# Every large SBUF buffer of a two-block transformer kernel placed at a multiple of 2048 bytes

## The chip, the cores and the metric

The kernel runs on one core of a Trainium2 chip. The metric is the device time of one launch in microseconds, median of the runs shown.

## The reference, cut to what matters

Two transformer blocks work on x of 512 rows by 1024 features in float32. The first has two layers: a norm, a projection, a gated spatial unit beside causal differential attention, an output projection, then a feed-forward part with a three-tap convolution. The second has one layer: a modulated norm, a projection, a linear recurrence beside sparse attention, an output projection, then a feed-forward part with a squared relu.

```python
for l in range(DEPTH):                                   # first block, DEPTH = 2
    proj = rmsnorm(h, attn_norm[l]) @ w_in[l]            # 1024 -> 2560
    mixed = concat([sgu_mixer(u, v_sgu, ...), diff_attention(q, k, v_att, ...)])
    h = h + mixed @ w_out[l]                             # 1024 -> 1024
    h = h + conv_ffn(rmsnorm(h, ffn_norm[l]), w_up[l], conv_w[l], conv_b[l], w_down[l])   # 1024 -> 2*2816, 2816 -> 1024
h = rmsnorm(h, final_norm)
y = hybrid_mixer(modulate(rms_norm(h, g), sh1, sc1), w_in_2, ..., w_out_2)                # second block
h = h + (1 + g1) * rms_norm(y, post_norm_mix_2)
y = square(relu(modulate(rms_norm(h, g), sh2, sc2) @ w_ff1_2)) @ w_ff2_2                  # 1024 -> 4096 -> 1024
return h + (1 + g2) * rms_norm(y, post_norm_mlp_2)
```

## The kernel before, in words

**Tiling.** Features lie on the 128 partitions, the 512 rows of x along a partition. So an activation tile is 128 x 512 float32, 2048 bytes of a partition. h holds the eight tiles of the residual stream.

**The product.** Every large matrix product is made of three matmuls in the reduced float32 format (`product`, L2024 to L2028): each operand is split into a high part and a low remainder, and high x high, high x low and low x high are summed in PSUM. Mostly the weight is the stationary operand (128 x 128) and the activation is streamed (512 columns).

```python
pe.matmul(out, l_hi, r_hi, start=start, stop=False)          # L2026
pe.matmul(out, l_hi, r_lo, start=False, stop=False)          # L2027
return pe.matmul(out, l_lo, r_hi, start=False, stop=stop)    # L2028
```

The profile names both inputs of a matmul in the order of the alphabet: `ps<-n_lo,w_hi` streams n_lo over the stationary w_hi. In some projections (forms `ps<-w_hi,n_hi`) the activation is stationary and the weight is streamed.

**The split operands.** n_hi and n_lo (8 tiles each) hold the normed activation that enters a projection or the upper half of a feed-forward part. x_hi and x_lo (4 tiles each) hold the gated result of the spatial unit, which enters the first half of the out-projection (`outs`; its second half `outa` reads n_hi and n_lo), and the hidden activation that enters the lower half of a feed-forward part.

**Weights.** SyncE loads a stripe of weights (1 MB or 512 KB) into raw0 or raw1, asked for when the stripe before it in that buffer has been split. A stripe has four quarters. ScalarE copies a quarter to w_hi (`hi`, L885), then POOL makes w_lo = raw - w_hi (`lo`, L848), into one of four slots. ScalarE runs three quarters ahead of PE (LOOK = 3), and a slot comes free when PE has done the quarter four before.

**The loops.** The feed-forward parts are hardware loops: 11 groups in each layer of the first block, 8 in the second. A turn does `up` for one group (four PSUM banks, 24 matmuls on n_hi and n_lo into each) and `down` for the group before (eight output tiles into four banks, 6 matmuls on x_hi and x_lo into each, 12 in the second block). VectorE and ScalarE turn the upper results into the hidden activation in zc (rb), ScalarE splits it to x_hi (L933), VectorE to x_lo (L1389), and VectorE adds the lower results to h (L1736) or y, which lies in zy (L1976).

**The layout.** `sb(name, shape)` takes SBUF from a stack: a buffer starts where the one before it ended, rounded up to 32 bytes, and a buffer opened in a `with ExitStack() as part` gives its place back, so that the next one lies over it. 1152 bytes of a partition are taken before the first buffer. Worked out from the shapes, a buffer's start counted past the last multiple of 2048, and past the last multiple of 64:

| buffers | before | of 64 | after | of 64 |
|---|---|---|---|---|
| raw0, raw1, w_hi, w_lo, h, n_hi, n_lo, zb, zc | 1152 | 0 | 0 | 0 |
| zd | 1152 | 0 | 0 | 0 |
| x_hi, x_lo, za, zy | 1696 | 32 | 0 | 0 |
| tb, cb_hi, sq | 128 | 0 | 0 | 0 |
| ss | 320 | 0 | 0 | 0 |
| blkw, rotF, cb_lo | 1632 | 32 | 0 | 0 |
| const | 320 | 0 | 448 | 0 |
| ones | 1920 | 0 | 1024 | 0 |

The buffers named are in `build` (L451 to L498 before the change). Tiles within the large buffers step by 2048 bytes, weight tiles within a slot by 512.

Of the kernel before, what the change touches and what calls it, by code (L numbers as in the profile page):

```python
# [19 lines left out]
F32 = mybir.dt.float32  # L20
F32R = mybir.dt.float32r
# [5 lines left out]
P = 128  # L27
S = 512
NT = S // P
D = 1024  # L30
DT = D // P
DEPTH = 2
HALF = D // 2
HT = HALF // P
HEADS = 4
FF = 2816
FG = FF // 256
# [70 lines left out]
NCONST = C_QSCALE + HEADS2 // 2  # L108
# [336 lines left out]
def build(nc, a):  # L445
# [7 lines left out]
    with ExitStack() as ctx:  # L453
        def sb(name, shape, dt=F32, where=ctx):
            return where.enter_context(nc.sbuf_tensor(name, shape, dt))
# [2 lines left out]
            return ctx.enter_context(nc.semaphore(name))  # L458


        raw = [sb(f"raw{i}", [P, 4096]) for i in range(2)]
        w_hi = sb("w_hi", [P, 4, 1024], F32R)
        w_lo = sb("w_lo", [P, 4, 1024], F32R)
# [4 lines left out]
        n_lo = sb("n_lo", [P, DT, S], F32R)  # L468
        zb = sb("zb", [P, 4096])
        zc = sb("zc", [P, 2048])  # L470
        zd = sb("zd", [P, 3328])
        with ExitStack() as part:
            tb = sb("tb", [P, 3, S], F32, part)
        cb_hi = sb("cb_hi", [P, 16, 64], F32R)
        sb("rest_of_tb", [P, S])
        sq = sb("sq", [P, 2, S])
        rt = sb("rt", [P, HEADS * NT])
        rstd = sb("rstd", [P, HEADS * NT + 1])
        ms = sb("ms", [P, 2 * NT])
        ss = sb("ss", [P, 2, S])  # L480
        const = sb("const", [P, NCONST])
        ones = sb("ones", [P, P])
        cols = sb("cols", [P, 6, P])
        par = sb("par", [P, DEPTH, FG * 16])
        cpar = sb("cpar", [P, 17])
        small = sb("small", [P, 48])
        more = sb("more", [P, 144])
        blkw = sb("blkw", [P, 2, HT, P])
        with ExitStack() as part:
            rotF = sb("rotF", [P, 2, S], F32, part)  # L490
        cb_lo = sb("cb_lo", [P, 16, 64], F32R)
        fgw = sb("fgw", [P, DT, 2])
        cw2 = [sb(f"cw2_{i}", [P, 2, P]) for i in range(2)]
        with ExitStack() as part:
            za = sb("za", [P, 4096], F32, part)
        x_hi = sb("x_hi", [P, 4, S], F32R)
        x_lo = sb("x_lo", [P, 4, S], F32R)
        zy = sb("zy", [P, 4096])  # L498
        banks = ctx.enter_context(nc.psum_tensor("ps", [P, 8 * S], F32))
        ps = [banks[:, i * S:(i + 1) * S] for i in range(8)]  # L500

# [2129 lines left out]
```

## Time and profile before

| what | value |
|---|---|
| median of 3 runs | 1925.64 us (1924.38 to 1927.17) |
| profiled execution, span from its first to its last instruction | 1919.2 us |
| what lies around that span, against the median | 6.4 us |
| TensorE busy | 1834.7 us, 96% of the span |
| VectorE, ScalarE, POOL busy | 54%, 41%, 46% |
| mean granted TensorE clock | 0.975 |
| HBM read | 180.42 MB, 95 GB/s over the span |

The profiled execution's time on the runs' clock is not listed apart; the median stands for it, and the span is what rows of the trace add up to. PE is TensorE's matmuls and PEld its weight loads, which overlap. Matmuls overlap one another as well: the start of the next, not the end, tells what one costs. A busy PE is not PE at its peak.

### The profile page before, as it was taken

How to read it: one execution, taken by the hardware profiler on the slowest of the kernel's cores; microseconds unless marked ns; L12 is line 12 of the kernel's file. 1: busy time of each engine (PE TensorE's matmuls, PEld its weight loads, DVE VectorE, ACT ScalarE, POOL GpSimd, SP SyncE). 2: the span in 40 equal slices, each digit the busy share in tenths (PEclk: the TensorE clock that was granted, in tenths of full speed). 3: DMA queues.
4: the chain of work that ended last, by engine and by line, in shares of the span. 5: the costliest groups of instructions: out<-in, count | busy, mean ns of one | idle time of the engine just before them, and what ended most of it. 6: DMA issues, size and time to landing. Idle time of an engine off the chain costs nothing.

```text
span 1919.2 us, 25690 instructions
## 1 busy us (share of the span) xinstructions
PE 1834.7 (96%) x8675; PEld 1466.2 (76%) x8675; DVE 1027.1 (54%) x1800; ACT 779.3 (41%) x1244; POOL 891.9 (46%) x1158
## 2 busy tenths in 40 slices
PE   7999999999999999999999999999988899999996
PEld 5767788888887877778888888867556778888885
DVE  4687556566656347576656654554675542222223
ACT  4434433333335334353333333485665342222223
POOL 5443345565555543255656554357112335555541
PEclk9999999999999999999999999899999789999998
DMA  7221224443322222124444323133001212223211
GB/s 240 89 88 44 77 67 153 142 153 127 135 88 88 90 87 74 36 78 142 153 142 153 135 95 110 51 105 126 8 1 45 88 44 88 87 92 120 94 44 44
DMA packets 102018, 183.43 MB, mean 96 GB/s; under 512 B 6794, under 2 KB 66748, under 8 KB 99900
## 3 DMA queue, kind: packets, MB, share of 16 engines
q1 hardware_dynamic: 101772, 181.80, 27.1%
q8 instruction: 40, 0.66, 0.1%
q10 hardware_dynamic: 176, 0.73, 0.1%
q14 instruction: 30, 0.25, 0.0%
HBM read 180.42 MB, written 2.10 MB: 95 GB/s over the span
## 4 chain that ended last, share of the span: by engine, by line
PE 87%; DVE 6%; ACT 3%; issue 3%; POOL 1%; DMA 0%; DVEq 0%; SPq 0%; ACTq 0%; POOLq 0%
PE ps L2026 26%; PE ps L2028 25%; PE ps L2027 25%; PE ps L2283 1%; DVE ss L1374 1%; PE ps L2052 1%; PE ps L2564 1%; PE ps L2220 1%; DVE n_lo L1393 1%; PE ps L2274 1%; DVE zy L1898 1%; PE ps L2537 1%; POOL w_lo L848 1%; PE ps L2513 1%; PE ps L2061 1%
## 5 line engine op out<-in xcount | busy, mean ns | idle before, releaser
L848 POOL TENSOR_TENSOR w_lo<-raw,w_hi 128x256 fp32r<-128x256 f32 (+1 forms) x1148 | 889.0, 807 | 989.1 <-ACT w_hi L885 988.9
L2026 PE MATMUL ps<-n_hi,w_hi 128*128 128x512 f32 x1432 | 573.6, 401 | 7.7 <-DVE n_lo L1411 3.2
L2028 PE MATMUL ps<-n_hi,w_lo 128*128 128x512 f32 x1432 | 561.3, 392 | 0.0
L2027 PE MATMUL ps<-n_lo,w_hi 128*128 128x512 f32 x1432 | 560.8, 392 | 0.0
L885 ACT ACTIVATE w_hi<-raw 128x1024 fp32r<-128x1024 f32 (+2 forms) x331 | 310.0, 944 | 302.5 <-PE ps L2028 183.8
L2026 PEld LDWEIGHTS ps<-n_hi,w_hi 128*128 128x128 f32 x1432 | 270.1, 189 | 69.2 <-issue 10.5
L2027 PEld LDWEIGHTS ps<-n_lo,w_hi 128*128 128x128 f32 x1432 | 270.2, 189 | 58.5 <-issue 4.3
L2028 PEld LDWEIGHTS ps<-n_hi,w_lo 128*128 128x128 f32 x1432 | 269.8, 188 | 59.0 <-issue 0.7
L2026 PE MATMUL ps<-x_hi,w_hi 128*128 128x512 f32 x672 | 272.5, 406 | 4.7 <-DVE x_lo L1389 4.7
L2027 PE MATMUL ps<-x_lo,w_hi 128*128 128x512 f32 x672 | 268.3, 399 | 0.0
L2028 PE MATMUL ps<-x_hi,w_lo 128*128 128x512 f32 x672 | 267.9, 399 | 0.0
L1718 DVE TENSOR_TENSOR ps<-ps,sq 128x512 f32<-128x512 f32 x88 | 61.4, 700 | 192.1 <-PE ps L2028 189.7
L2026 PEld LDWEIGHTS ps<-x_hi,w_hi 128*128 128x128 f32 x672 | 127.9, 190 | 39.1 <-DVE x_lo L1389 5.3
L1088 ACT ACTIVATE zc<-ps,cpar 128x512 f32<-128x512 f32 x88 | 68.2, 775 | 210.9 <-DVE ps L1718 210.9
L2028 PEld LDWEIGHTS ps<-x_hi,w_lo 128*128 128x128 f32 x672 | 127.9, 190 | 31.6
L1736 DVE TENSOR_TENSOR h<-h,ps 128x512 f32<-128x512 f32 x176 | 111.3, 679 | 75.3 <-PE ps L2028 75.3
L2027 PEld LDWEIGHTS ps<-x_lo,w_hi 128*128 128x128 f32 x672 | 128.2, 191 | 29.6 <-issue 0.5
L1976 DVE TENSOR_TENSOR zy<-zy,ps 128x512 f32<-128x512 f32 x64 | 41.4, 683 | 140.3 <-PE ps L2028 140.3
L1971 DVE TENSOR_TENSOR zc<-zc 128x512 f32<-128x512 f32 x32 | 23.8, 745 | 123.7 <-ACT zc L1322 123.7
L933 ACT ACTIVATE x_hi<-zc 128x512 fp32r<-128x512 f32 x76 | 43.2, 624 | 70.6 <-PE ps L2028 68.6
L1725 DVE SCALAR_TENSOR_TENSOR zc<-ps,cpar,zc 128x510 f32<-128x510 f32 x88 | 65.9, 749 | 3.1
L1389 DVE TENSOR_TENSOR x_lo<-zc,x_hi 128x512 fp32r<-128x512 f32 x76 | 65.6, 910 | 0.2
(285 smaller groups left out, 1886.5 us busy)
## 6 DMA issues: line engine op xcount, KB each, us to landing
raw<-in_w_up SPq DMA_DIRECT2D x44, 1024.0 KB, 6.8
raw<-in_w_ff SPq DMA_DIRECT2D x32, 1024.0 KB, 6.3
raw<-in_w_in SPq DMA_DIRECT2D x26, 1024.0 KB, 7.1
zb<-in_ada_w SPq DMA_DIRECT2D x16, 1536.0 KB, 7.9
raw<-in_w_down SPq DMA_DIRECT2D x44, 512.0 KB, 4.0
raw<-in_w_out SPq DMA_DIRECT2D x12, 1024.0 KB, 6.0
raw<-in_w_in SPq DMA_DIRECT2D x4, 512.0 KB, 10.1
za<-in_x SPq DMA_DIRECT2D x4, 512.0 KB, 7.9
```

The source lines that it names most:

```text
L848: last = pool.tensor_tensor(parts[0][:, c], parts[1][:, c], parts[2][:, c], ALU.subtract)
L885: act.activation(split_quarter(st.kind, w_hi, g % 4, q), raw_quarter(st.kind, raw[st.index % 2], q), ACT.Copy).then_inc(whi_ready, 1)
L933: act.activation(dst, src, ACT.Copy).then_inc(hi_ready, 1)
L1088: act.activation(rb[t], ps[t][:, :], ACT.Identity, bias=cpar[:, 4 * t + 3:4 * t + 4], scale=cpar[:, 4 * t + 2:4 * t + 3]).then_inc(conv_be ...
L1389: dve.tensor_tensor(lo_, src, hi_, ALU.subtract).then_inc(lo_ready, 1)
L1718: dve.tensor_tensor(ps[t][:, :], ps[t][:, :], factor, ALU.mult).then_inc(up_scaled, 1)
L1725: dve.scalar_tensor_tensor(rb[t][:, 2:S], ps[t][:, 0:S - 2], cpar[:, 4 * t:4 * t + 1], rb[t][:, 2:S], ALU.mult, ALU.add).then_inc(free[t], 1)
L1736: dve.tensor_tensor(h[:, m, :], h[:, m, :], ps[4 + m % 4][:, :], ALU.add)\
L1976: dve.tensor_tensor(y[:, m, :], y[:, m, :], ps[4 + m % 4][:, :], ALU.add)\
L2026: pe.matmul(out, l_hi, r_hi, start=start, stop=False)
L2027: pe.matmul(out, l_hi, r_lo, start=False, stop=False)
L2028: return pe.matmul(out, l_lo, r_hi, start=False, stop=stop)
```

## The change

The seven small buffers of parameters and of norm results are opened first, with a filler of 88 floats that nothing uses: 64 + 96 + 32 + 96 + 192 + 64 + 352 = 896 bytes after the 1152, so raw0 starts at 2048. After them come the buffers whose sizes are multiples of 2048 bytes, then zd and the remaining parameters. za with x_hi and x_lo, and zy, move ahead of tb. Sizes, pairs that share a place, and all instructions stay.

```diff
@@ -458,6 +458,13 @@
             return ctx.enter_context(nc.semaphore(name))
 
 
+        rt = sb("rt", [P, HEADS * NT])
+        rstd = sb("rstd", [P, HEADS * NT + 1])
+        ms = sb("ms", [P, 2 * NT])
+        cpar = sb("cpar", [P, 17])
+        small = sb("small", [P, 48])
+        fgw = sb("fgw", [P, DT, 2])
+        sb("to_tiles", [P, 88])
         raw = [sb(f"raw{i}", [P, 4096]) for i in range(2)]
         w_hi = sb("w_hi", [P, 4, 1024], F32R)
         w_lo = sb("w_lo", [P, 4, 1024], F32R)
@@ -468,34 +475,28 @@
         n_lo = sb("n_lo", [P, DT, S], F32R)
         zb = sb("zb", [P, 4096])
         zc = sb("zc", [P, 2048])
-        zd = sb("zd", [P, 3328])
+        with ExitStack() as part:
+            za = sb("za", [P, 4096], F32, part)
+        x_hi = sb("x_hi", [P, 4, S], F32R)
+        x_lo = sb("x_lo", [P, 4, S], F32R)
+        zy = sb("zy", [P, 4096])
         with ExitStack() as part:
             tb = sb("tb", [P, 3, S], F32, part)
         cb_hi = sb("cb_hi", [P, 16, 64], F32R)
         sb("rest_of_tb", [P, S])
         sq = sb("sq", [P, 2, S])
-        rt = sb("rt", [P, HEADS * NT])
-        rstd = sb("rstd", [P, HEADS * NT + 1])
-        ms = sb("ms", [P, 2 * NT])
         ss = sb("ss", [P, 2, S])
-        const = sb("const", [P, NCONST])
-        ones = sb("ones", [P, P])
-        cols = sb("cols", [P, 6, P])
-        par = sb("par", [P, DEPTH, FG * 16])
-        cpar = sb("cpar", [P, 17])
-        small = sb("small", [P, 48])
-        more = sb("more", [P, 144])
         blkw = sb("blkw", [P, 2, HT, P])
         with ExitStack() as part:
             rotF = sb("rotF", [P, 2, S], F32, part)
         cb_lo = sb("cb_lo", [P, 16, 64], F32R)
-        fgw = sb("fgw", [P, DT, 2])
+        zd = sb("zd", [P, 3328])
         cw2 = [sb(f"cw2_{i}", [P, 2, P]) for i in range(2)]
-        with ExitStack() as part:
-            za = sb("za", [P, 4096], F32, part)
-        x_hi = sb("x_hi", [P, 4, S], F32R)
-        x_lo = sb("x_lo", [P, 4, S], F32R)
-        zy = sb("zy", [P, 4096])
+        ones = sb("ones", [P, P])
+        cols = sb("cols", [P, 6, P])
+        par = sb("par", [P, DEPTH, FG * 16])
+        more = sb("more", [P, 144])
+        const = sb("const", [P, NCONST])
         banks = ctx.enter_context(nc.psum_tensor("ps", [P, 8 * S], F32))
         ps = [banks[:, i * S:(i + 1) * S] for i in range(8)]
```

## Rows read from the trace of the kernel before

**Rows 1.** The page: busy time by engine (share, instructions), and the chain that ended last.

```profile
PE 1834.7 (96%) x8675; PEld 1466.2 (76%) x8675; DVE 1027.1 (54%) x1800; ACT 779.3 (41%) x1244; POOL 891.9 (46%) x1158
...
PE 87%; DVE 6%; ACT 3%; issue 3%; POOL 1%; DMA 0%; DVEq 0%; SPq 0%; ACTq 0%; POOLq 0%
PE ps L2026 26%; PE ps L2028 25%; PE ps L2027 25%; PE ps L2283 1%; DVE ss L1374 1%; PE ps L2052 1%; PE ps L2564 1%; PE ps L2220 1%; DVE n_lo L1393 1%; PE ps L2274 1%; DVE zy L1898 1%; PE ps L2537 1%; POOL w_lo L848 1%; PE ps L2513 1%; PE ps L2061 1%
```

**Rows 2.** Table of stretches, the three feed-forward loops: us, busy (instructions), clock, DMA.

```profile
core 0: us, PE busy (x) PEld busy (x) DVE busy (x) ACT busy (x) POOL busy (x), PEclk, DMA share, GB/s
255.00:590.00 335.00, 335.00 (x1463) 273.42 (x1462) 206.94 (x272) 122.07 (x167) 182.90 (x243) 1.00 0.35 121
845.00:1190.00 345.00, 344.54 (x1508) 281.47 (x1507) 210.91 (x279) 125.07 (x172) 188.27 (x248) 1.00 0.36 124
1550.00:1875.00 325.00, 325.00 (x1415) 265.00 (x1413) 80.17 (x118) 93.99 (x120) 170.44 (x236) 1.00 0.23 84
sum 1005.00, PE 1004.54 PEld 819.89 DVE 498.03 ACT 341.13 POOL 541.62; mean PE 334.85 PEld 273.30 DVE 166.01 ACT 113.71 POOL 180.54
```

**Rows 3.** Groups of PE's instructions: line, form xcount | busy us, mean ns | idle before.

```profile
L2026 PE MATMUL ps<-n_hi,w_hi 128*128 128x512 f32 x1432 | 573.6, 401 | 7.7 <-DVE n_lo L1411 3.2 <-DVE n_lo L1389 2.2 <-issue 1.4
L2028 PE MATMUL ps<-n_hi,w_lo 128*128 128x512 f32 x1432 | 561.3, 392 | 0.0
L2027 PE MATMUL ps<-n_lo,w_hi 128*128 128x512 f32 x1432 | 560.8, 392 | 0.0
L2026 PE MATMUL ps<-x_hi,w_hi 128*128 128x512 f32 x672 | 272.5, 406 | 4.7 <-DVE x_lo L1389 4.7
L2027 PE MATMUL ps<-x_lo,w_hi 128*128 128x512 f32 x672 | 268.3, 399 | 0.0
L2028 PE MATMUL ps<-x_hi,w_lo 128*128 128x512 f32 x672 | 267.9, 399 | 0.0
L2026 PE MATMUL ps<-w_hi,n_hi 128*128 128x512 f32 x128 | 52.2, 408 | 5.5 <-issue 3.7 <-DVE zd L1470 1.8
L2027 PE MATMUL ps<-w_lo,n_hi 128*128 128x512 f32 x128 | 51.4, 402 | 0.0
L2028 PE MATMUL ps<-w_hi,n_lo 128*128 128x512 f32 x128 | 51.4, 402 | 0.0
```

**Rows 4.** Timeline of PE, second block's loop: start us, duration us, engine, line, operation.

```profile
1698.35 0.40 PE L2026 MATMUL ps<-n_hi,w_hi 128*128 128x512 f32 x1
...
1719.92 0.39 PE L2028 MATMUL ps<-n_hi,w_lo 128*128 128x512 f32 x1
1720.15 0.40 PE L2026 MATMUL ps<-x_hi,w_hi 128*128 128x512 f32 x1
...
1742.32 0.40 PE L2028 MATMUL ps<-x_hi,w_lo 128*128 128x512 f32 x1
```

**Rows 5.** Timeline of PE, out-projection of layer 0: on x, then on n.

```profile
204.89 0.39 PE L2027 MATMUL ps<-x_lo,w_hi 128*128 128x512 f32 x1
...
207.22 0.39 PE L2028 MATMUL ps<-x_hi,w_lo 128*128 128x512 f32 x1
...
221.07 0.39 PE L2026 MATMUL ps<-n_hi,w_hi 128*128 128x512 f32 x1
...
231.72 0.39 PE L2028 MATMUL ps<-n_hi,w_lo 128*128 128x512 f32 x1
```

**Rows 6.** Two stretches at the halved clock: table of stretches, then PE's timeline.

```profile
211.00:214.00 3.00, 3.00 (x8) 2.42 (x9) 0.00 (x0) 0.26 (x1) 0.00 (x0) 0.50 0.00 0
1488.00:1490.00 2.00, 2.00 (x6) 1.52 (x6) 1.97 (x4) 1.58 (x2) 1.58 (x2) 0.50 0.00 0
...
212.03 0.63 PE L2028 MATMUL ps<-x_hi,w_lo 128*128 128x512 f32 x1
...
213.31 0.63 PE L2028 MATMUL ps<-x_hi,w_lo 128*128 128x512 f32 x1
...
1488.11 0.63 PE L2028 MATMUL ps<-n_hi,w_lo 128*128 128x512 f32 x1
...
1489.82 0.63 PE L2026 MATMUL ps<-n_hi,w_hi 128*128 128x512 f32 x1
```

**Rows 7.** Groups of VectorE and ScalarE whose operands lie at different places.

```profile
L1736 DVE TENSOR_TENSOR h<-h,ps 128x512 f32<-128x512 f32 x176 | 111.3, 679 | 75.3 <-PE ps L2028 75.3
L1976 DVE TENSOR_TENSOR zy<-zy,ps 128x512 f32<-128x512 f32 x64 | 41.4, 683 | 140.3 <-PE ps L2028 140.3
...
L908 ACT ACTIVATE sq<-h 128x512 f32<-128x512 f32 x28 | 17.3, 621 | 7.9 <-DVE h L1602 4.7 <-DVE ss L1374 3.1
L908 ACT ACTIVATE sq<-zy 128x512 f32<-128x512 f32 x14 | 8.7, 626 | 15.8 <-DVE zy L1976 9.9 <-DVE zy L1942 5.8
...
L933 ACT ACTIVATE x_hi<-tb 128x512 fp32r<-128x512 f32 x8 | 5.1, 634 | 21.6 <-DVE tb L1593 21.6
L933 ACT ACTIVATE n_hi<-tb 128x512 fp32r<-128x512 f32 x16 | 10.1, 631 | 25.4 <-DVE tb L1608 21.0 <-DVE tb L1874 2.8 <-DVE tb L1419 1.4
...
L1389 DVE TENSOR_TENSOR x_lo<-tb,x_hi 128x512 fp32r<-128x512 f32 x8 | 5.5, 684 | 0.0
L1389 DVE TENSOR_TENSOR n_lo<-tb,n_hi 128x512 fp32r<-128x512 f32 x16 | 11.9, 743 | 1.4 <-ACT n_hi L933 1.3
```

**Rows 8.** POOL: its group on the page, its wait (us, times, longest), its timeline.

```profile
L848 POOL TENSOR_TENSOR w_lo<-raw,w_hi 128x256 fp32r<-128x256 f32 (+1 forms) x1148 | 889.0, 807 | 989.1 <-ACT w_hi L885 988.9
...
POOL w_lo L848 <- ACT w_hi L885: 988.9, 215, 37.9
...
1711.09 2.83 POOL L848 TENSOR_TENSOR w_lo<-raw,w_hi 128x256 fp32r<-128x256 f32 x4 [1.52 <-ACT w_hi L885]
1716.53 2.83 POOL L848 TENSOR_TENSOR w_lo<-raw,w_hi 128x256 fp32r<-128x256 f32 x4 [2.62 <-ACT w_hi L885]
```

**Rows 9.** The chain in order of time, its first transfer; PE's wait for it.

```profile
1.32 6.68 DMA za<-in_x
...
PE ps L2158 <- DMA za<-in_x: 8.1, 1, 8.1
```

## The prediction, made before the result was known

> **What bounds the kernel now.** Four views, in this order. The page's busy shares and chain [rows 1]: TensorE (PE) is busy 1834.7 of the span's 1919.2 us and makes 87% of the chain that ended last; three source lines alone, the three matmuls of one compensated float32 product (L2026 to L2028), make 76% of it. The table of stretches [rows 2]: in the two feed-forward loops of the first block and in the one of the second, 1005 us together, PE is busy for 1004.5 us at a granted clock of 1.00, while POOL, the next busiest, has 541.6 us. So in those stretches the time is the number of matmuls times the distance from one start to the next, and no wait stands in it. The groups of product matmuls [rows 3] split this work by what they stream: 4680 stream n_hi, n_lo or, with n as the stationary side, w_hi and w_lo (3 x 1432 + 3 x 128); 2016 stream x_hi or x_lo (3 x 672). Of the three costliest forms the first kind shows 401, 392 and 392 ns for one, the second 406, 399 and 399. These durations overlap, so they are only a hint. The timeline gives the real price [rows 4]: in one turn of the second block's loop 96 matmuls on n start from 1698.35 to 1719.92 us, 21.57 us over 95 steps, 227.1 ns each; the next 96, on x, start from 1720.15 to 1742.32 us, 22.17 us over 95 steps, 233.4 ns each. Both have 512 columns and a 128x128 stationary tile, with nothing idle between.
>
> What differs is where the streamed operand lies. By the layout, n_hi, n_lo, w_hi and w_lo begin 1152 bytes past a multiple of 2048, which is a multiple of 64 (and 128); x_hi and x_lo begin at 1696, which is 32 past a multiple of 64. Two other differences could stand behind the 6.3 ns: the upper loop half sums 24 matmuls into a PSUM bank, the lower half 6 or 12. Here the trace has a control [rows 5]: the two halves of the out-projection use the same weight layout and 12 matmuls per bank, one on x, one on n. On x, 10 steps take 2.33 us (233 ns); on n, 47 steps take 10.65 us (226.6 ns). So the price goes with the operand, not with the grouping.
>
> **The change, part by part.** (1) The streamed x_hi and x_lo move from 32 past a multiple of 64 to a multiple of 2048. Their distance in phase to w_hi and w_lo becomes zero, just as n_hi's is now, so the nearest row for them is n's 227.1 ns. Gain: 233.4 - 227.1 = 6.3 ns, times 2016 = 12.7 us. The page's means give a second road: 5 + 7 + 7 = 19 ns for each triple, times 672 = 12.8 us. Subtractions: at the halved clock (0.50 in these windows) x steps by 1.28 us in 3 (427 ns) and n by 1.71 in 4 (427 ns) [rows 6], so the few dozen x matmuls that run there gain nothing, some 0.2 us; and the 192 x matmuls of the two attention stages stand in short runs between softmax steps, where VectorE and ScalarE set part of the pace, so I take off half of their 1.2 us. Left: 12.7 - 0.2 - 0.6 = 11.9 us.
>
> (2) Everything else that is large moves from 1152 to 0 past a multiple of 2048. No row has n at another phase. Bounds: nothing lower than the halved clock's 427 ns divided by two, 213.5 ns, is thinkable for 512 columns, which would be 13.6 ns less on each of 4680; upward, n could cost what x costs now, 6.3 ns more. I take 0, because 1152 and 0 are both multiples of 64 and 128, and n keeps its phase to the weights.
>
> (3) The engines beside PE. VectorE's sum with a PSUM operand takes 679 ns on h and 683 on zy, which lies at 1696 like x; ScalarE's square 621 from h, 626 from zy; its copy 634 into x_hi and 631 into n_hi; VectorE's difference 684 for x_lo, 743 for n_lo [rows 7]. So these engines see no price in the place beyond 5 ns, and the parameters, read a few columns at a time, are taken at 0. POOL's part takes 2.83 us per quarter of weights, while PE spends 24 x 227 ns = 5.4 us on one, and it waits for ScalarE before nearly each [rows 8]; even 1 us more per quarter stays hidden there. If that cover were gone, a w_lo late by 0.1 us in each of 287 quarters (1148 instructions, four to one) would cost 29 us, but after this change a lower-half quarter of 12 x 227 ns = 2.7 us is only 0.08 us shorter than now, with three quarters of run-ahead kept. Late next, if anything, is w_lo in that half: the change takes 48 x 6.3 = 0.3 us from a turn, which is no wait.
>
> (4) The transfers. All but the first are asked for stripes ahead. At the start PE waits 8.1 us for x in za, of which 6.68 us is the transfer [rows 9]. za moves from 160 past a multiple of 256 to a multiple of it. No row has another phase; bounds by the rows are a tenth of 6.68 us each way, and I take 0.
>
> Sum: -11.9 us. Against the profiled execution's own span that is 1919.2 - 11.9 = 1907.3 us. The median of the runs, 1925.64, lies 6.4 us above the span, and that part (launch and end) is untouched: 1913.7 us. A measurement of this kernel can tell about 0.2%, 3.9 us, from no change.
>
> **The rivals.** *No effect of address.* The 6.3 ns would come from the work, say the PSUM banks' order or VectorE beside the lower half. Against it stands the control [rows 5]; for it, that the x runs there are short. Time: 1925.6 us. The Trainium skill (SBUF — State Buffer, the note on cachelines) speaks for this rival: a consecutive read pays only for each new line of 16 bytes, and 1696 and 1152 are both multiples of 16; by that rule nothing changes. The trace's 233.4 beside 227.1 ns do not agree with it.
>
> *More than x.* The 13.6 ns between 227.1 and 213.5 would also be an address price, which the full 2048 removes from all 6696: 4680 x 13.6 = 64 us and 2016 x 19.9 = 40 us, so 1822 us. For it: at the halved clock no such surcharge shows. Against: n's streams and w's, a run of 512 and one of 128 columns at different offsets, all sit at 227 already. The Trainium skill (TensorE: Matmul & The Clock Gate, Back-to-back issue gap) gives N/2.4 + 2.5 ns for isolated matmuls, 216 ns here; by that the sum would be an estimated 1925.6 - 87 = 1838 us. The trace shows 227.1 with a weight load before each matmul.
>
> *Slower: a common phase.* Now x stands apart from the weights and the other buffers; afterwards PE's stream, its weight load and the other engines' operands all begin at one phase, where they may collide. Place: the product matmuls; price: n's 4680 at x's 6.3 ns more, 29.5 us, with x kept at 233.4: 1955 us. It decides from 11.9 / 4680 = 2.5 ns per n matmul. Against it: n_hi, raw, h and w_hi share one phase already, and they are the fast ones.
>
> **How the numbers follow.** Forecast 0.82 (two roads to its term and a control); no effect 0.08; more 0.05; slower 0.05. Forecast's own spread: 6.3 ns may be 5 (some of the x steps follow a stall) or 7.1, plus 0.7 us of the transfer and 1.5 us of scatter: 1909 to 1918. Stretched to take in half-effects, 1907 to 1920. Faster by over 0.2%: 0.82 and 0.05, less a little for a half-effect, 0.86; within: 0.09; slower: 0.05.
>
> **What would show it.** In the profile of the changed kernel the x block of a turn should step by 227 ns as the n block does, L2027 and L2028 on x should have n's mean of about 392 ns, and a turn of the second block's loop, 44.2 us from one n block's start to the next's (192 steps), should take 43.6. n's step and the means of POOL, VectorE and ScalarE should stay within 1%. The prediction is wrong if x keeps 233 ns, if n's step moves by more than 1 ns, or if a wait for w_lo or x_lo appears inside the loops.

## The result, and the profile of the changed kernel

The changed kernel took 1909.86 us in the median (4 runs, 1907.88 to 1910.30), the kernel before 1926.41 us beside it (4 runs, 1924.38 to 1928.69): a ratio of 0.9913, 95% interval [0.9896, 0.9930], or 16.5 us less. The forecast was 1913.7 us in 1907 to 1920. A second comparison, with nine runs of the changed kernel and fourteen of the one before, gave a little less: 1914.68 against 1927.0 us, 0.9938 [0.9917, 0.9959], 12.3 us. Both hold; why they differ, and how much of either is the layout's, comes with the experiments.

The page of the changed kernel, same parts as [rows 1], and its groups of product matmuls beside [rows 3]. All source lines are one further down, so L2026 to L2028 are now L2027 to L2029; the chain's first three entries are still these.

```profile
span 1908.2 us, 25690 instructions
PE 1823.5 (96%) x8675; PEld 1465.1 (77%) x8675; DVE 1031.8 (54%) x1800; ACT 779.6 (41%) x1244; POOL 884.4 (46%) x1158
...
PE 87%; DVE 6%; ACT 3%; issue 3%; POOL 1%; DMA 0%; DVEq 0%; SPq 0%; ACTq 0%; POOLq 0%
...
L849 POOL TENSOR_TENSOR w_lo<-raw,w_hi 128x256 fp32r<-128x256 f32 (+1 forms) x1148 | 881.5, 803 | 985.4 <-ACT w_hi L886 983.7
L2027 PE MATMUL ps<-n_hi,w_hi 128*128 128x512 f32 x1432 | 572.9, 400 | 7.7 <-DVE n_lo L1412 3.2
L2029 PE MATMUL ps<-n_hi,w_lo 128*128 128x512 f32 x1432 | 561.2, 392 | 0.0
L2028 PE MATMUL ps<-n_lo,w_hi 128*128 128x512 f32 x1432 | 560.7, 392 | 0.0
...
L2027 PE MATMUL ps<-x_hi,w_hi 128*128 128x512 f32 x672 | 269.0, 400 | 4.7 <-DVE x_lo L1390 4.7
L2028 PE MATMUL ps<-x_lo,w_hi 128*128 128x512 f32 x672 | 264.2, 393 | 0.0
L2029 PE MATMUL ps<-x_hi,w_lo 128*128 128x512 f32 x672 | 264.0, 393 | 0.0
```

The same instructions, 11.0 us less span (1919.2 to 1908.2), and PE's busy time is 11.2 us less. The x groups went from 406, 399 and 399 ns to 400, 393 and 393; the n groups stayed where they were. POOL did not slow down (807 to 803 ns). Since a matmul's duration overlaps the next one's, the price is read from the distance between starts, in the timeline of PE in the second block's loop, as in [rows 4]: 96 starts on x, then 96 on n, then the next block on x and the next on n.

```profile
1711.53 0.39 PE L2027 MATMUL ps<-x_hi,w_hi 128*128 128x512 f32 x1
...
1733.06 0.39 PE L2029 MATMUL ps<-x_hi,w_lo 128*128 128x512 f32 x1
1733.29 0.39 PE L2027 MATMUL ps<-n_hi,w_hi 128*128 128x512 f32 x1
...
1754.82 0.39 PE L2029 MATMUL ps<-n_hi,w_lo 128*128 128x512 f32 x1
...
1776.81 0.39 PE L2027 MATMUL ps<-n_hi,w_hi 128*128 128x512 f32 x1
```

Each block takes 21.53 us over 95 steps, 226.7 ns, on x as on n. Before, it was 233.4 on x and 227.1 on n. A turn, from one n block's start to the next's, takes 43.52 us (1733.29 to 1776.81) where it took 44.20.

The table of stretches answers to [rows 2]; the stretch of the second block is set a little earlier, since the program has reached it earlier.

```profile
core 0: us, PE busy (x) PEld busy (x) DVE busy (x) ACT busy (x) POOL busy (x), PEclk, DMA share, GB/s
255.00:590.00 335.00, 335.00 (x1469) 274.71 (x1468) 208.80 (x273) 122.28 (x168) 181.20 (x244) 1.00 0.35 122
840.00:1180.00 340.00, 340.00 (x1495) 278.93 (x1493) 212.43 (x278) 125.44 (x171) 182.71 (x246) 1.00 0.35 124
1540.00:1860.00 320.00, 320.00 (x1414) 264.96 (x1413) 83.66 (x123) 95.59 (x122) 167.74 (x233) 1.00 0.24 85
sum 995.00, PE 995.00 PEld 818.60 DVE 504.89 ACT 343.32 POOL 531.65; mean PE 331.67 PEld 272.87 DVE 168.30 ACT 114.44 POOL 177.22
```

PE is busy in every microsecond of it. That hides something: 1463 instructions in 335 us became only 1469, 0.4% more. With the x third of them 2.9% quicker one would look for about 1%. The timeline shows what is in the way. PE with its weight loads, and VectorE, in a turn of the first block's loop, at the 25th matmul on x (column in brackets: idle before it and what ended that).

```profile
290.15 1.87 DVE L1737 TENSOR_TENSOR h<-h,ps 128x512 f32<-128x512 f32 x3
...
290.56 0.39 PE L2029 MATMUL ps<-x_hi,w_lo 128*128 128x512 f32 x1
290.88 0.19 PEld L2027 LDWEIGHTS ps<-x_hi,w_hi 128*128 128x128 f32 x1 [0.35 <-DVE h L1737]
290.88 0.50 PE L2027 MATMUL ps<-x_hi,w_hi 128*128 128x512 f32 x1
...
291.22 0.39 PE L2028 MATMUL ps<-x_lo,w_hi 128*128 128x512 f32 x1
```

The same place in the kernel before:

```profile
290.21 1.87 DVE L1736 TENSOR_TENSOR h<-h,ps 128x512 f32<-128x512 f32 x3
...
290.77 0.40 PE L2028 MATMUL ps<-x_hi,w_lo 128*128 128x512 f32 x1
...
290.94 0.19 PEld L2026 LDWEIGHTS ps<-x_hi,w_hi 128*128 128x128 f32 x1 [0.21 <-DVE h L1736]
291.01 0.44 PE L2026 MATMUL ps<-x_hi,w_hi 128*128 128x512 f32 x1
...
291.29 0.39 PE L2027 MATMUL ps<-x_lo,w_hi 128*128 128x512 f32 x1
```

Here the fifth output tile starts in the PSUM bank of the first, and VectorE must first have added that bank to h. VectorE's chain did not get quicker, PE did: the two steps around this matmul are 0.32 and 0.34 us after the change, 0.24 and 0.28 before, instead of 0.227 each. PE still counts as busy, because the last matmul's modelled end covers the gap. Summed over the 20 turns of both loops the excess of these two steps over 227 ns is 4.08 us, against 0.94 before: 3.1 us of the gain were given back in a wait that the prediction said would not come. The steps right behind it are longer too (236, 231, 233 and 231 ns as medians of the turns, then 227 again), which brings the loss near 4 us.

The account by stage, from the starts of the same instructions in both traces: the two loops of the first block, each with the last group of `down` behind it, 3.3 us less each, the second block 4.4, the attention stages and the start 0 within 0.2 us. From the steps: 1922 x matmuls at full clock by 6.0 ns (233.4 to 227.35, short stalls included) are 11.6 us; n's 4477 by 0.2 ns are 0.9; less 3.1 that is 9.4 us.

The rest of the 11.0 us is the clock. Of the first block's 3.3 us the ten turns of a loop give only 1.5 to 1.6; the last group behind them gives 1.7, of which its own shorter steps are at most 0.3. There, behind some 3 us of small matmuls of a norm, PE ran on at the halved clock in the profiled execution of the kernel before (the third number from the right is the granted clock):

```profile
597.00:599.00 2.00, 2.00 (x6) 1.52 (x6) 0.00 (x0) 0.00 (x0) 0.88 (x2) 0.50 0.00 0
1187.00:1189.00 2.00, 2.00 (x5) 1.63 (x6) 0.00 (x0) 0.00 (x0) 1.18 (x2) 0.50 0.00 0
```

and at the full clock in that of the changed kernel:

```profile
595.50:597.50 2.00, 2.00 (x10) 1.63 (x9) 0.00 (x0) 0.00 (x0) 0.84 (x2) 1.00 0.08 5
1182.50:1184.50 2.00, 2.00 (x10) 1.67 (x9) 0.00 (x0) 0.00 (x0) 0.87 (x2) 1.00 0.07 6
```

These two places are worth 2.9 us; behind the second block's loop the halved stretch is longer in the changed kernel, which costs it 1.0. With the 9.4 that makes 11.3, beside the 11.0 measured. In its second profile the changed kernel is at the halved clock behind the second loop as well (0.50 from 1190.50 to 1192.50 us), so this part differs between executions of one kernel and is not shown to come from the layout. About 9 of the 11.0 us are the layout's.

### The profile page after: what moved, and what is told of

The parts are those of the page before. It is cut to its first block, busy times and chain, and to the rows that moved or that the text cites. A ratio compares the mean times of both kernels' runs of the same rounds, so it can differ in the third digit from the quotient of the medians.

```text
span 1908.2 us, 25690 instructions
## 1 busy us (share of the span) xinstructions
PE 1823.5 (96%) x8675; PEld 1465.1 (77%) x8675; DVE 1031.8 (54%) x1800; ACT 779.6 (41%) x1244; POOL 884.4 (46%) x1158
## 4 chain that ended last, share of the span: by engine, by line
PE 87%; DVE 6%; ACT 3%; issue 3%; POOL 1%; DMA 0%; DVEq 0%; SPq 0%; ACTq 0%; POOLq 0%
PE ps L2027 26%; PE ps L2028 25%; PE ps L2029 25%; PE ps L2284 1%; DVE ss L1375 1%; PE ps L2053 1%; PE ps L2565 1%; DVE n_lo L1394 1%; PE ps L2221 1%; PE ps L2275 1%; DVE zy L1899 1%; PE ps L2538 1%; POOL w_lo L849 1%; PE ps L2514 1%; PE ps L2062 1%
## 5 line engine op out<-in xcount | busy, mean ns | idle before, releaser
L2027 PE MATMUL ps<-n_hi,w_hi 128*128 128x512 f32 x1432 | 572.9, 400 | 7.7 <-DVE n_lo L1412 3.2
L2029 PE MATMUL ps<-n_hi,w_lo 128*128 128x512 f32 x1432 | 561.2, 392 | 0.0
L2028 PE MATMUL ps<-n_lo,w_hi 128*128 128x512 f32 x1432 | 560.7, 392 | 0.0
L2027 PEld LDWEIGHTS ps<-n_hi,w_hi 128*128 128x128 f32 x1432 | 270.2, 189 | 69.0 <-issue 10.5
L2028 PEld LDWEIGHTS ps<-n_lo,w_hi 128*128 128x128 f32 x1432 | 270.1, 189 | 58.1 <-issue 4.3
L2029 PEld LDWEIGHTS ps<-n_hi,w_lo 128*128 128x128 f32 x1432 | 269.7, 188 | 58.3 <-issue 0.8
L2027 PE MATMUL ps<-x_hi,w_hi 128*128 128x512 f32 x672 | 269.0, 400 | 4.7 <-DVE x_lo L1390 4.7
L2028 PE MATMUL ps<-x_lo,w_hi 128*128 128x512 f32 x672 | 264.2, 393 | 0.0
L2029 PE MATMUL ps<-x_hi,w_lo 128*128 128x512 f32 x672 | 264.0, 393 | 0.0
L2027 PEld LDWEIGHTS ps<-x_hi,w_hi 128*128 128x128 f32 x672 | 127.7, 190 | 38.4 <-DVE h L1737 7.1
L2029 PEld LDWEIGHTS ps<-x_hi,w_lo 128*128 128x128 f32 x672 | 127.6, 190 | 27.4
L2028 PEld LDWEIGHTS ps<-x_lo,w_hi 128*128 128x128 f32 x672 | 127.6, 190 | 25.8 <-issue 0.5
L1390 DVE TENSOR_TENSOR x_lo<-zc,x_hi 128x512 fp32r<-128x512 f32 x76 | 69.8, 964 | 0.2
```

Source lines behind the costliest of these rows:

```text
L1390: dve.tensor_tensor(lo_, src, hi_, ALU.subtract).then_inc(lo_ready, 1)
```

## The experiments

In these experiments fillers in the layout change, or the place of one addition in VectorE's order, or both; each kernel does the whole computation. "Distance" is the start of the streamed operand in a partition minus the start of the weights, modulo 256 bytes. Before, it was 0 for n and 32 for x (1696 - 1152 = 544 = 2 x 256 + 32).

**How firm is the 16.5 us.** The changed kernel again, in nine runs.

> The changed kernel itself once more, to measure the size. If the gain is only the shorter step of x (some 2000 matmuls by 6 ns, less a wait), it is 11 to 12 us, ratio 0.994. If the first comparison's 16.5 us are real, a second cause exists beside the step of x and this comparison gives 15 to 18 us again, ratio 0.991 to 0.992.

It gave 1914.68 us (1906.94 to 1921.25, 9 runs) against 1927.0 (1921.52 to 1931.73, 14 runs), ratio 0.9938 [0.9917, 0.9959]. The runs scatter by more than they did in the first comparison, and they do so with the granted clock: the 9 runs go from 1906.94 us at a mean clock of 0.981 to 1921.25 at 0.971. Over the 67 runs of this study that list a clock and have a fellow run, each kernel about its own mean, one thousandth of mean clock goes with 1.4 us (scatter left about that line: 1.4 us). Set to a clock of 0.975 by this slope, an estimate, the kernel before takes 1922.8 +- 0.3 us and the changed one 1914.4 +- 0.5 here, 1912.2 +- 0.7 in the first comparison. At equal clock, then, the layout is worth 8 to 11 us, about the 9.4 of the account; the rest is that the changed kernel happened to run, or was made to run, at a clock of 0.974 to 0.977 in the mean, the other at 0.971 to 0.973. Which of the two is left open; the slowest layouts below ran at 0.975 to 0.977, so the clock does not simply follow x's step.

**Is it the place or the distance.** Three layouts. In the first, the kernel before with eight words in front of x, x lies at 1728, a multiple of 64, and everything else stays:

```diff
         cw2 = [sb(f"cw2_{i}", [P, 2, P]) for i in range(2)]
+        sb("pad", [P, 8])
         with ExitStack() as part:
```

> The kernel before with 32 bytes of filler ahead of za: x_hi, x_lo, za and zy start at 1728 past a multiple of 2048 (a multiple of 64, not of 128), all else stays at 1152. Theory A (x's start past a multiple of 64 is the whole cause): x steps by 227 ns and the time is that of the changed kernel within 0.1%. Theory B (the full 2048, or 128, is needed): x keeps 233 ns and the time that of the kernel before. Theory C (more than x): x steps by 227 ns and the time lies between the two, some 5 us above the changed kernel.

In the second, the changed kernel with every large buffer at 32 past a multiple of 2048, distances 0:

```diff
-        sb("to_tiles", [P, 88])
+        sb("to_tiles", [P, 96])
```

> The changed kernel with every large buffer 32 bytes further, so that weights, n and x share one phase, 32 past a multiple of 64. If the place itself counts, n and x both step by 233 ns: 6696 matmuls by 6.3 ns, 40 us slower than the changed kernel. If only the distance in phase between the streamed and the stationary operand counts, both step by 227 ns and nothing changes.

In the third, the changed kernel with the weights alone moved by 32 bytes; x, n and all else stay on multiples of 2048:

```diff
+        sb("pad0", [P, 8])
         w_hi = sb("w_hi", [P, 4, 1024], F32R)
         w_lo = sb("w_lo", [P, 4, 1024], F32R)
+        sb("pad1", [P, 8])
```

> The changed kernel with 32 bytes of filler ahead of w_hi and 32 behind w_lo: the weights start 32 past a multiple of 64, n, x and all else at a multiple of 64. If the distance between the streamed and the stationary operand counts, every product that streams n or x is 32 off: 6312 matmuls by 6.5 ns, about 40 us slower than the changed kernel, steps of 233 ns on n and on x. If only the streamed operand's own place counts (against the run with all buffers at 32), steps stay at 227 ns.

Measured: 1916.25 us (6 runs), 0.9944 [0.9926, 0.9962] for the first; 1913.09 (4 runs), 0.9924 [0.9899, 0.9948] for the second; 1949.1 (2 runs), 1.0114 [1.0076, 1.0151] for the third. The timelines of PE say what happened to the step. x at a multiple of 64 with the weights at 1152:

```profile
1714.66 0.40 PE L2027 MATMUL ps<-x_hi,w_hi 128*128 128x512 f32 x1
...
1736.42 0.39 PE L2029 MATMUL ps<-x_hi,w_lo 128*128 128x512 f32 x1
```

Everything at 32:

```profile
1714.69 0.39 PE L2027 MATMUL ps<-x_hi,w_hi 128*128 128x512 f32 x1
...
1736.23 0.39 PE L2029 MATMUL ps<-x_hi,w_lo 128*128 128x512 f32 x1
```

The weights alone at 32, first the block on x, then the one on n:

```profile
1698.19 0.40 PE L2029 MATMUL ps<-x_hi,w_hi 128*128 128x512 f32 x1
...
1720.35 0.39 PE L2031 MATMUL ps<-x_hi,w_lo 128*128 128x512 f32 x1
1720.59 0.40 PE L2029 MATMUL ps<-n_hi,w_hi 128*128 128x512 f32 x1
...
1742.75 0.40 PE L2031 MATMUL ps<-n_hi,w_lo 128*128 128x512 f32 x1
```

Over 95 steps these are 21.76 us (229.1 ns), 21.54 us (226.7), and 22.16 us on both x and n (233.3). The second says that the place of an operand does not count: x at 32 past a multiple of 64 is as quick as anywhere. The third says that the distance does: x and n, both on multiples of 2048, became slow because the weights moved, and the kernel is 22 us slower than the one before with an alignment that looks nearly perfect. The first says that 64 is not the unit: a multiple of 64 still pays 2.4 ns.

**What the unit is.** Six more layouts. x was put 16 bytes, 128 bytes and 256 bytes further in the changed kernel (a filler of 32 or 64 words in front of za; the 16 bytes by a slice of a larger buffer); in two kernels, which also have the earlier addition of the experiment after this one, n was moved as well; and last the kernel before got a filler of 224 bytes, to bring x to 768 bytes past the weights' phase:

```diff
         cw2 = [sb(f"cw2_{i}", [P, 2, P]) for i in range(2)]
+        sb("pad", [P, 56])
         with ExitStack() as part:
```

> The changed kernel with za, x_hi and x_lo 16 bytes further (zy and what follows 64 further). The rule of 16-byte lines gives 227 ns a step for x. Lines of 64 bytes, or any dependence on the distance to the weights, give 230 to 236 ns.

> The changed kernel with 128 bytes of filler ahead of za: x is a multiple of 128 away from the weights' phase, but not of 256. The distance of 64 gave 229 ns. If the period is 128, x steps by 227 ns here; if it is longer (256, 512), by 228 to 231 ns; a step below 226.7 ns would be a better place than the common phase.

> As the run with 128 bytes, with 256: 227 ns if the period is 256 or less, above 228 if it is longer.

> On top of the run that adds first: n_hi and n_lo 192 bytes past the weights' phase, x_hi and x_lo 224. Distances so far: 0 and 256 gave steps of 226.7 ns, 16 gave 231.6, 32 gave 233.4, 64 gave 229.1, 128 gave 233.2, and weights 32 ahead of the streamed operand (a distance of 224) 233.3. If the distance within 256 bytes decides, x steps by 233 ns here. For n at 192: by symmetry with 64, 229 ns; a step near 213 ns would be a better place than the common phase.

> As before with n at 96 and x at 160. By symmetry the two give about the same step, between 229 and 234 ns. A step below 226.7 would overturn that the common phase is best.

> The kernel before with 224 bytes of filler ahead of za and nothing else: x_hi and x_lo start at 1920 past a multiple of 2048, a distance of 768 = 3 x 256 from the weights' phase, while everything else stays at 1152. If the distance within 256 bytes is the whole cause, x steps by 226.7 ns, the wait at the fifth output tile is 4 us in all, and the time is that of the changed kernel within the scatter (12 us under the kernel before at equal clock it would be 8 to 11). If the round places themselves give something, the changed kernel stays some us faster.

Times, in that order: 1922.71, 1923.93, 1907.98, 1947.81 and 1950.66 us (one run each) and 1916.51 us (5 runs) against 1926.32, 0.9946 [0.9932, 0.9960]. Blocks on x in the timeline of PE at 16, 128 and 256 bytes, each from its own kernel. At 16, where x is a slice of the buffer x_all:

```profile
1722.55 0.39 PE L2028 MATMUL ps<-x_all,w_hi 128*128 128x512 f32 x1
...
1744.55 0.40 PE L2030 MATMUL ps<-x_all,w_lo 128*128 128x512 f32 x1
```

At 128:

```profile
1723.16 0.40 PE L2028 MATMUL ps<-x_hi,w_hi 128*128 128x512 f32 x1
...
1745.33 0.39 PE L2030 MATMUL ps<-x_hi,w_lo 128*128 128x512 f32 x1
```

At 256:

```profile
1709.19 0.39 PE L2028 MATMUL ps<-x_hi,w_hi 128*128 128x512 f32 x1
...
1730.72 0.39 PE L2030 MATMUL ps<-x_hi,w_lo 128*128 128x512 f32 x1
```

22.00, 22.17 and 21.53 us: 231.6, 233.4 and 226.6 ns. All layouts together, x's or n's mean step in the second block's loop:

| distance, bytes mod 256 | step, ns | kernels |
|---|---|---|
| 0 (0, 256 and 768) | 226.7 | changed, all at 32, x at 256, filler of 224 |
| 16 | 231.6 | x at 16 |
| 32 | 233.4 | before |
| 64 | 229.1 | x at 64 |
| 96 | 233.3 | n at 96 |
| 128 | 233.3 | x at 128 |
| 160 | 234.2 | x at 160 |
| 192 | 233.3 | n at 192 |
| 224 | 233.3 | x at 224; weights at 32 |

So the step is at its lowest where stream and weights begin at the same place modulo 256 bytes; 16 bytes away it costs 4.9 ns more, and most other distances cost the 6.6 ns that the kernel before paid. One value between is quicker than its neighbours, 64, with 229.1. And since the filler of 224 bytes does to x's step all that the change does, 226.7 ns, nothing of the change's other moves was needed for it.

The forms that stream the weights over a stationary n (`ps<-w_hi,n_hi`) check the table, since there the distance has the opposite sign. With n at 96 it is 160, and their full-speed steps take 233.7 to 234.3 ns in every stretch, as x's at 160. With n at 192 it is 64, and two of the three long stretches take 228.9 ns, as x's at 64, but the third, from 673.0 to 695.2 us, 233.3. So the 160 repeats, and 64 is not always the quicker value. What in the chip makes this distance count is not shown by any of these runs, and distances that are no multiple of 16 were not tried.

**The wait for the bank.** If the new wait is VectorE's first add coming late, it must vanish when that add stands earlier in VectorE's order. In the changed kernel it stood behind the last product of the convolution, which itself waits for ScalarE; now it stands ahead of that product:

```diff
-                def conv_steps(j):
+                def conv_steps(j, between=None):
...
+                        if i == 1 and between is not None:
+                            between()
                         dve.wait_ge(free[2 * i + 1], n0[2 * i + 1] + j + 1)
...
-                        conv_steps(j)
-                        down_steps(gq + 4 + 8 * (j - 1))
+                        conv_steps(j, lambda: down_steps(gq + 4 + 8 * (j - 1), None, range(1)))
+                        down_steps(gq + 4 + 8 * (j - 1), None, range(1, DT))
```

> The changed kernel, with VectorE's first addition of the lower half's result (the one that frees the bank of the fifth output tile) moved ahead of its last product of the convolution part, in the two loops of the first block. If the wait of PE at the fifth output tile, about 0.2 us in each of 20 turns, is for VectorE's first addition, it goes and the time falls by 3 to 4 us. If it is for something else (weights), it stays and nothing changes or the later x_hi costs something.

> The changed kernel with the first addition moved ahead, once more: 4 us under the changed kernel at equal granted clock, ratio to the kernel before 0.990 to 0.993, and about 4 us under the run with 224 bytes of filler of the same call.

The two comparisons gave 1912.38 us (6 runs), 0.9910 [0.9889, 0.9932], and 1911.51 us (5 runs) against 1926.32, 0.9930 [0.9916, 0.9943]. The timeline of the second, at the same place of the turn:

```profile
288.71 0.68 DVE L1738 TENSOR_TENSOR h<-h,ps 128x512 f32<-128x512 f32 x1
289.31 0.68 DVE L1732 TENSOR_TENSOR zc<-zc 128x512 f32<-128x512 f32 x1
289.91 2.04 DVE L1738 TENSOR_TENSOR h<-h,ps 128x512 f32<-128x512 f32 x3
...
290.23 0.39 PE L2030 MATMUL ps<-x_hi,w_lo 128*128 128x512 f32 x1
...
290.46 0.39 PE L2028 MATMUL ps<-x_hi,w_hi 128*128 128x512 f32 x1
...
290.69 0.39 PE L2029 MATMUL ps<-x_lo,w_hi 128*128 128x512 f32 x1
```

The first add, now ahead of the convolution's product (zc<-zc), begins 1.75 us before the 25th matmul (290.46), where in the changed kernel it began 0.73 before it (290.15 and 290.88), and PE steps by 0.23 us. From one such matmul to that of the next turn it is 33.03 us in the kernel before, 32.87 in the changed one and 32.64 here, as means over the turns of both loops (the first: 291.01 to 324.03, 290.88 to 323.76, 290.46 to 323.10): of the 0.39 us that a turn of the first block can gain, the changed kernel got 0.16, and the wait with the longer steps behind it costs it 0.23, 4.7 us in 20 turns. The excess of the two steps alone over the 20 turns is 0.0 us in both profiles with the earlier addition, against 4.08 in the changed kernel, 4.06 in its second profile and 4.11 with the 224-byte filler. Against the kernels with the wait on the same chips the medians fell by 2.3 us (1914.68 to 1912.38) and by 5.0 (1916.51 to 1911.51); the intervals of the ratios still overlap, so the times alone do not settle it. At a clock of 0.975 it is 4.2 us (1914.4 to 1910.2) and 5.5 (1915.0 to 1909.5), which agrees with the 4.7 us of the turns within the error of about 0.8. The mechanism is shown by the timelines. This is the quickest version: at equal clock 12.6 to 13.3 us below the kernel before.

## Why the prediction was right, and where its steps were not

**(1) x's step: size and sign right, the cause misnamed.** Forecast 6.3 ns on each of 2016; measured 6.7 in the second block's loop and 6.0 over all full-speed steps, 11.6 us. The control of [rows 5] was good: operand, not grouping. But the prediction explained the 6.3 ns by x beginning 32 past a multiple of 64, and used the distance to the weights only as a second remark. The runs show the second remark to be the whole: all buffers at 32 keep 226.7 ns, weights moved alone make 233.3 of it, and a multiple of 64 pays 229.1. The trace of before could not tell these apart, since there x was off in both senses; a text that said so would have been the better one. The forecast came out because the change sets both right at once.

**The 0.6 us of the attention stages: wrong.** Half of x's gain there was booked; the stages did not get shorter (0 within 0.2 us). That fits stages paced by the softmax steps, which no run tests; the whole gain should have been struck.

**(2) n and the weights moved from 1152 to 0, taken at 0: right.** 227.05 to 226.66 ns in the loop. The 0.4 ns are those of the first steps behind an x block, which before started out of the regular pattern of 227, 227, 226 ns; over all of n's matmuls it is 0.9 us that was not forecast.

**(3) The other engines: the prices named right but one, what is late next wrong.** VectorE's sum on h kept 679 ns and ScalarE's square on zy 626, as [rows 7] had let expect, and POOL's w_lo was in time. But VectorE's means did not all stay within 1%: its costliest difference, x_lo from zc, which [rows 7] leave out, rose from 910 to 964 ns (76 of them, 4.2 us), and n_lo from 743 to 757. The first follows the timing and not the place: it is 964 as well with the 224-byte filler, 911 with the weights at 32 and 842 with the earlier addition. PE's waits for x_lo are 4.7 us before and after, so no delay of PE by it shows. Nor did [rows 7] bear out "no price beyond 5 ns": they have 684 ns for x_lo beside 743 for n_lo, which was not explained. But "late next, if anything, is w_lo in that half", with no wait, is the step that failed: late next was PSUM bank 4, released by VectorE's first add: 3.1 us at the two steps around it, near 4 with those behind. The trace of before already had the row, a weight load with 0.21 us of idle ended by that add; it was missed because the three loops looked free of waits at PE's busy share of 1.00, and because only the second block's loop, which has no convolution, was read turn by turn.

**(4) The transfers, taken at 0: right.** PE's first wait went from 8.1 us to 7.9, and za's transfer from 6.68 us to 6.40, with 6.81 in the second profile of the changed kernel.

**The sum: some 1 to 4 us too high at equal clock, its base misread.** Forecast 11.9 us; the two profiled spans differ by 11.0, of which 1.9 are stretches at the halved clock (means 0.975 and 0.976), and equal-clock times by 8 to 11. The bank wait is the larger part of that. As its base the prediction put the 1925.64 of the median as "6.4 us above the span, launch and end". It isn't: every run of the study that lists both has its time 2.0 to 2.1 us above its span. The other 4.3 us are that the profiled execution of before lay low in its own scatter, at a clock of 0.975 where the fourteen runs of the second comparison have 0.972 in the mean. So the scatter, set at 1.5 us, was too small. The first comparison's 16.5 us against the forecast's 11.9 comes from this scatter, and not from the steps. The range was not met by luck alone: 1914.68 of the second comparison lies in it as well, and the prediction's main term was measured. But that the first time lies 3.8 us below the forecast and not a little above it is the clock of those four runs (0.976 to 0.979); at equal clock the layout gives less than was forecast.

**The rivals.** *No effect of address* fell: x's step moved with a filler of 224 bytes alone. It had the rule of the Trainium skill behind it (SBUF — State Buffer, cachelines of 16 bytes); the trace disagrees for a matmul, where a shift of 16 bytes costs 4.9 ns. *More than x* fell: n stays at 226.7 ns wherever the buffers lie together. The Trainium skill (TensorE: Matmul & The Clock Gate, Back-to-back issue gap) gives 216 ns for isolated matmuls and about 131 for a sustained stream of weight loads and matmuls; no stretch of this kernel's product matmuls at the full clock reaches either, the best is 226.7. *Slower: a common phase* had it the wrong way round: the common phase is the best place found, and it is a phase apart that is 6.6 ns slower.

## What to carry to other kernels

Where a matmul stream sets the time, read the step from start to start for each operand, and place the streamed and the stationary operand at the same address modulo 256 bytes; aligning each by itself to some round number is not what counts, and moving the weights alone by 32 bytes took the changed kernel from 1914.68 to 1949.1 us. When the bounding engine is made quicker by some per cent, look at every bank or buffer that another engine hands back to it just in time, in each kind of loop, in the timeline and not by the busy share. Set a forecast against a run's own time and granted clock, since here a thousandth of mean clock went with 1.4 us.

## What was not expected of the hardware

- A compensated float32 matmul of 512 columns steps by 226.7 ns with stream and weights 0, 256 or 768 bytes apart, by 231.6 at 16, 229.1 at 64 and 233.3 to 234.2 at all other distances tried (table above; at 64 one stretch of streamed weights took 233.3). At the halved clock of the kernel before, x at 32 and n at 0 both step by 427 ns [rows 6].
- The steps at distance 0 repeat as 227, 227, 226 ns; at 32 they spread over 230 to 235 ns, at 64 over 226, 229 and 232, at 128 they alternate between 229 and 238.
- Time follows the mean granted clock within one kernel, 1.4 us per thousandth. From the steps, an estimate: a microsecond at the halved clock lowers the mean by 0.5/1920 = 0.00026 and costs 1 - 227/427 = 0.47 us of matmuls, so 1.8 us per thousandth where PE sets the pace. Whether a layout changes how often the clock falls is left open: the changed kernel's runs had 0.974 to 0.977 in the mean, those of the kernel before 0.971 to 0.973.
